# Sums of expert rows on TensorE, weight pieces into the slot that is free first, and overflow blocks in pairs

## The reference

```
# top-1 of 4 groups, then top-2 of its 8 experts; 32 experts, each 1024 -> 512 -> 1024, per layer
weights = p_group * top_p / sum(top_p)                     # two numbers for each token
y = (silu(xb @ w1[e]) * (xb @ w3[e])) @ w2[e]              # for each row given to expert e
out = sum over the token's two experts of  y * weight
x  <- LayerNorm(alpha * x + gate * out) * ln_w + ln_b      # alpha = (2 * DEPTH) ** 0.25
```

## Time and profile before

| | |
|---|---|
| median of 3 launches | 2706.59 us (2704.28 to 2708.8) |
| the profiled execution | 2711.27 us |
| its span, first to last instruction | 2709.4 us |
| PE busy | 2269.5 us (84%) |
| DVE busy | 823.1 us (30%) |
| ACT busy | 445.1 us (16%) |
| POOL busy | 352.8 us (13%) |
| mean granted clock of PE | 0.916 of full |

### The profile page before, as it was taken

How to read it: one execution, slowest core, us unless ns; L and a number is a source line. 1 busy time by engine, 2 the same in 40 slices (tenths; PEclk the granted TensorE clock), 3 DMA queues, 4 the chain that set the end, 5 groups by cost and what they waited for, 6 DMA issues and landing times.

```text
span 2709.4 us, 28307 instructions
## 1 busy us (share of the span) xinstructions
PE 2269.5 (84%) x10288; PEld 1147.0 (42%) x10288; DVE 823.1 (30%) x1648; ACT 445.1 (16%) x956; POOL 352.8 (13%) x341
## 2 busy tenths in 40 slices
PE   7989999998958898999940999998958898998920
PEld 3555458884543343433310444443543343433410
DVE  2764135554342011111139201102351111110147
ACT  2201234441211111111111100000111110111111
POOL 0000123221210000000015000001210000000025
PEclk8999999999978999999975999998968998999965
DMA  9861000003255989899852301102065989899743
GB/s 388 324 241 36 0 1 2 2 2 111 75 213 231 421 358 422 344 420 414 334 194 97 88 23 46 46 0 78 31 265 223 422 362 416 345 420 421 311 173 149
DMA packets 135164, 572.21 MB, mean 211 GB/s; under 512 B 24153, under 2 KB 49913, under 8 KB 82554
## 3 DMA queue, kind: packets, MB, share of 16 engines
q1 hardware_dynamic: 121786, 536.92, 50.3%
q0 software_dynamic: 13248, 33.57, 3.2%
HBM read 549.47 MB, written 35.65 MB: 216 GB/s over the span
## 4 chain that ended last, share of the span: by engine, by line
PE 63%; DMA 15%; DVE 11%; SPq 5%; issue 3%; ACT 1%; POOL 1%; POOLq 0%; DVEq 0%; ACTq 0%
PE bank L966 14%; PE bank L1038 12%; DMA bigA<-in_moe_w 9%; PE bank L988 8%; PE bank L606 7%; PE bank L876 4%; PE bank L898 4%; SPq L392 4%; PE bank L709 3%; DMA bigC<-in_moe_w 2%; DVE lnwb L1365 2%; PE bank L563 2%; DVE bigA L1781 2%; DVE bigA L1783 2%; SPq L508 2%
## 5 line engine op out<-in xcount | busy, mean ns | idle before, releaser
L966 PE MATMUL bank<-bigA,bigB 128*32 128x512 f32 (+2 forms) x1920 | 476.1, 624 | 28.7 <-DMA bigA<-in_moe_w 25.4
L1038 PE MATMUL bank<-bigB,bigA 128*128 128x512 f32 x768 | 331.6, 595 | 4.9 <-DMA bigA<-in_w_in_odd 4.9
L606 PE MATMUL bank<-bigC,bigB 128*128 128x512 f32 (+3 forms) x768 | 291.8, 535 | 0.4 <-ACT bigB L1075 0.4
L988 PE MATMUL bank<-bigA,bigB 128*32 128x512 f32 (+2 forms) x1040 | 268.1, 608 | 18.9 <-DMA bigA<-in_moe_w 9.7
L966 PEld LDWEIGHTS bank<-bigA,bigB 128*32 128x32 f32 (+2 forms) x1920 | 166.3, 143 | 273.3 <-issue 268.3
L966 PE MATMUL bank<-bigC,bigB 128*32 128x512 f32 (+2 forms) x768 | 244.8, 631 | 32.1 <-DMA bigA<-in_moe_w 15.3
L1038 PEld LDWEIGHTS bank<-bigB,bigA 128*128 128x128 f32 x768 | 146.5, 191 | 189.3 <-issue 189.3
L606 PEld LDWEIGHTS bank<-bigC,bigB 128*128 128x128 f32 x768 | 142.0, 192 | 127.5 <-issue 119.4
L1075 ACT ACTIVATE bigB<-bank,small 128x128 f32<-128x128 f32 x288 | 106.6, 460 | 475.5 <-PE bank L563 475.5
L1915 POOL TENSOR_TENSOR bigA<-bigA,lnwb 128x1024 f32<-128x1024 f32 x32 | 81.9, 2558 | 700.6 <-ACT bigA L1203 700.6
L1931 POOL DMA_INDIRECT y_rows<-bigB,ints x44 | 44.3, 1007 | 966.4 <-DVE bigB L1738 966.4
(11 more groups left out here) (263 smaller groups left out, 2293.0 us busy)
## 6 DMA issues: line engine op xcount, KB each, us to landing
bigA<-in_moe_w SPq DMA_DIRECT2D x288, 1024.0 KB, 24.1
bigC<-in_moe_w SPq DMA_DIRECT2D x96, 1024.0 KB, 16.7
bigA<-in_ada_w SPq DMA_DIRECT2D x40, 1024.0 KB, 7.8
bigA<-y_rows SPq DMA_DIRECT2D x16, 1024.0 KB, 4.8
bigA<-in_w_in_odd SPq DMA_DIRECT2D x24, 512.0 KB, 5.5
bigA<-in_ada_w SPq DMA_DIRECT2D x4, 2048.0 KB, 12.4
bigA<-in_x SPq DMA_DIRECT2D x16, 512.0 KB, 11.1
bigC<-in_w_in_even SPq DMA_DIRECT2D x4, 2048.0 KB, 13.7
```

The lines of the kernel that those rows point to most:

```text
L606: last = mm(bank(n % 3)[:, 0:w], uT[:, k, t * P:(t + 1) * P], wring[:, g % 2, k, at_:at_ + w], start=(k == 0), stop=(k == KC - 1))
L966: last = mm(bank(m)[at_:at_ + w, :], xT[:, j, KC // 2 * h + k, at_:at_ + w], w13_at[SLOT_OF[m, h, q][0]][:, k, :], start=(h == 0 and k == ...
L988: last = mm(bank(6 + n)[at_:at_ + w, :], gT[:, 2 * h + k, at_:at_ + w], w2_at[SLOT_OF[2, h, q][0]][:, k, n * 512:(n + 1) * 512], start=(h ...
L1038: last = mm(bank(3 * half + m), wc[:, j, m, k, :], u1T[:, k, half * 512:(half + 1) * 512], start=(k == 0), stop=(k == KC - 1))
```

## The change

1. **Slots.** A piece goes to the slot that comes free first by the plan, no longer to slot n % 16. `BEFORE[n]` is the piece that held it, and SP waits for the end of that one. The order of the pieces stays.
2. **Sums on PE.** The gate is multiplied into the rows before they are scattered: DVE alone takes both halves of a block's result from PSUM, times `gate`. In the tail PE forms alpha * hback + weight0 * row0 + weight1 * row1 in PSUM, by six matmuls a tile: against alpha times the identity (`alpha_i`) and against diagonal tiles of the weights (`share`), which POOL makes by 16 instructions at the start of each expert loop. DVE takes the statistics from PSUM, ACT normalises from PSUM, and DVE instead of POOL does the product with `ln_w` and the sum with `ln_b` (`affine`).
3. **Order of the tail of layer 0.** The transposes and the modulation of tile t - 2 are put in after the sum of tile t (`stream_T`), where they stood behind all sums on ACT and DVE. They use banks 0 to 3 of PSUM.
4. **Overflow loop.** 12 turns with one test on every engine, SP too; a turn would take two blocks.
5. **SP** issues the first two loads of `hback` before its overflow loop, and behind it waits for the last scatters itself instead of for POOL.

```diff
-SLOT_OF = {piece: (n % SLOTS, n // SLOTS) for n, piece in enumerate(PIECES)}
+def freed(piece):
+    m, h, q = piece
+    return (LAST[q], 2 * m + h) if m < 2 else (LAST[q] + 1, 4)
+
+SLOT_OF, BEFORE, FILLS, _held = {}, {}, [0] * SLOTS, []
+for _n, _piece in enumerate(PIECES):
+    _slot = _n
+    if _n >= SLOTS:
+        _, _, _slot, BEFORE[_n] = _held.pop(0)
+    SLOT_OF[_piece] = (_slot, FILLS[_slot])
+    FILLS[_slot] += 1
+    _held = sorted(_held + [(freed(_piece), _n, _slot, _piece)])
...
-            with eng.Fori(0, (OVER + 1) // 2) as i:
-                for j in range(2):
-                    with eng.If(2 * i + j < n_over):
+            with eng.Fori(0, OVER // 2) as i:
+                with eng.If(2 * i < n_over):
+                    for j in range(2):
                         block_(i + NB // 2, j)
...
-                        m_was, h_was, q_was = PIECES[n - SLOTS]
+                        m_was, h_was, q_was = BEFORE[n]
...
+                for t in range(2):
+                    load(hback[:, t], h_dram[l][t * P:(t + 1) * P, :], f"pair_in{t}")
-                with sp.Fori(0, OVER) as o:
-                    with sp.If(o < n_over):
+                with sp.Fori(0, OVER // 2) as i:
+                    with sp.If(2 * i < n_over):
...
-                sp.wait_ge(S("rows_out"), l + 1)
+                for j in range(2):
+                    sp.wait_ge(S(f"y_out{j}"), 16 * (NB // 2) * (l + 1))
...
@@ tensor @@
+            def combined(l, t):
+                if t == 0:
+                    pe.wait_ge(S("share_ok"), l + 1)
+                pe.wait_ge(S(f"pair_in{t % 2}"), 32 * (NT // 2 * l + t // 2 + 1))
+                if t >= 2:
+                    pe.wait_ge(S("nrm"), NT * (2 * l + 1) + t - 1)
+                for n in range(2):
+                    cols_n = slice(n * 512, (n + 1) * 512)
+                    dst = bank(4 + 2 * (t % 2) + n)
+                    mm(dst, alpha_i[:, :], hback[:, t % 2, cols_n], start=True, stop=False)
+                    for k in range(2):
+                        last = mm(dst, share[:, k, t, :], pair[:, t % 2, k, cols_n], start=False, stop=(k == 1))
+                last.then_inc(S("comb"), 1)
...
             for t in range(NT):
-                pe.wait_ge(S("ln"), NT + t + 1)
+                combined(0, t)
                 if t >= 2:
-                    pe.wait_ge(S("tile_a"), NT + t - 1)
-                    pe.wait_ge(S("tile_d"), NT + t - 1)
-                transposes(hh[:, t], 4 + 2 * (t % 2)).then_inc(S("tile_T"), 1)
+                    stream_T(t - 2)
...
@@ scalar @@
-                    go(yo[:, j, 0:512], bank(6), ACT.Copy).then_inc(S(f"y_ev{l}"), 1)
...
@@ vector @@
-                    v.tensor_copy(yo[:, j, 512:1024], bank(7)).then_inc(S(f"y_ev{l}"), 1)
+                    for n in range(2):
+                        v.tensor_tensor(yo[:, j, n * 512:(n + 1) * 512], bank(6 + n), gate[:, 1, n * 512:(n + 1) * 512], MUL)\
+                            .then_inc(S(f"y_ev{l}"), 1)
...
-                    V(v.tensor_scalar(z, pair[:, j, 0, :], wts[:, 0, t:t + 1], None, MUL))
-                    V.wait()
-                    V(v.scalar_tensor_tensor(z, pair[:, j, 1, :], wts[:, 1, t:t + 1], z, MUL, ADD))
-                    V.wait()
-                    V(v.tensor_tensor(z, z, gate[:, 1, :], MUL))
-                    V.wait()
-                    v.scalar_tensor_tensor(z, hback[:, j], ALPHA, z, MUL, ADD).then_inc(S("comb"), 1)
...
             for t in range(NT):
-                dve.wait_ge(S("tile_T"), NT + t + 1)
-                modulated(u1T[:, :, t * P:(t + 1) * P], 4 + 2 * (t % 2), mod_of(1, 0), "tile_d")
+                combined(0, t)
+                if t >= 2:
+                    stream_T(t - 2)
+                affine(0, t)
...
@@ gpsimd @@
                 gather(1, tok[:, 1:2])
+                for k in range(2):
+                    for t in range(NT):
+                        last = pool.tensor_scalar(share[:, k, t, :], ident, wts[:, k, t:t + 1], None, MUL)
+                last.then_inc(S("share_ok"), 1)
```

124 lines of the change are left out of this document (73 added, 51 removed).

## The result

The changed kernel takes **2561.8 us** (median of 4 runs, 2561.2 to 2566.1) where the kernel before takes 2707.4 (4 runs, 2704.3 to 2708.8): a ratio of 0.947, with an interval of 0.945 to 0.948. That is 145.6 us less; 132 were forecast, and 2561.8 lies in the range of 2552 to 2604. The profiled execution took 2561.2 us with a span of 2559.4.

What follows compares the result with a forecast made beforehand. PE was taken to bound the loops, idling 41.5 us a layer for weights, and DVE the tails. Gains of 56 (loops), 36.4 and 40 (tails) sum to 132 us, from 2706.6 to 2575, range 2552 to 2604.

Steps and rivals of the forecast that it cites:

- The holes in the loop: Expert loops: four stretches with DMA nearly idle, 36 us in layer 0, all gone once pieces take the first free slot.
- The carried table: Layer 0's expert loop: event times computed by recurrences from trace rows, with old and new slot releases; loop ends 1379 and 1350.
- the term of 28 us a layer: Expert loops: gain from the new slots, 29 us carried, taken as 28; 56 us for two layers, from 36 to 80.
- The bound of 18 us: Expert loops: lower bound of the slots' gain per layer, if each gather and scatter costs the queues twice as much.
- Rival D: Expert loops: gathers starve in always-full queues and the kernel is slower than before; 2785 at 39 us landing time; chance 0.02.
- rival A: Expert loops: holes close but little comes of it, 10 us for both layers; 2621 us; chance 0.12.
- The cover for what moved into the loop: Expert loops: DVE's extra 15 us and POOL's 9.6 us of diagonal tiles hide and cost nothing; uncovered, 10 us a layer.
- The pace: Tails: time per tile falls from 10.84 us to 6.1, or 6.3 in layer 0; bounds 5.9 and 7.0.
- The chain 2.28 + 1.3 + 2.5: Tails, one tile: statistics to ACT's product, ACT's product, then DVE's two wide instructions, with gaps; 6.1 us.
- one test less saves about a quarter, 8.7 us: Start of layer 0's tail: DVE's 12 overflow turns, 12.1 us with two tests, take 8.7 us with one.
- The write of the last tile behind it stays: End of layer 1's tail: the last tile's write after the last affine step stays, so no gain there (0 us).
- Rival B: Tails: PE's sums run at 1.2 GHz, 10.3 us each, and PE becomes the bound; 2652 us; chance 0.04.

Runs made afterwards that it cites:

- old-walk kernel: Kernel after with 12 overflow turns of two tests, SP's 24 turns, SP waiting for POOL, and rows of h loaded behind the loop; 2580.7 us (0.952).

## Why the prediction was right, point by point

**The holes in the loop: right, its size a little small.** The step "all four holes are gone" is in the row of 40 slices, and the slots alone give it. The carried table held within 1 us in all rows that were looked up but one: the last w2 piece of block 3 at 941 (trace 940.0), the last piece of all at 1330 (1330.3), the loop's end at 1350 (1349.6), and the outputs put at 921, 1063 and 1274 end at 920.4, 1063.6 and 1273.7. (By its numbers these are the outputs computed in the steps of blocks 3, 9 and 18, so those of blocks 2, 8 and 17. The exception is the 1296 of block 18: its own last w2 piece lands at 1291.1; the one that lands at 1296.1 belongs to the expert of blocks 19 to 21.) Some of this is luck, since everything began 1.8 us sooner than in the table: counted from the loop's start, the trace is 1 to 2.5 us behind it. What was mis-sized is the term of 28 us a layer, which measured 30.6 and 32.5. The carried loop was 3 us short for the kernel *before* (1379 against 1382), and I took a microsecond off the gain for it. The error was in the carried old loop alone. From its start at 833.4 the carried new loop is 516.6 us long, and measured were 518.0 and 516.2; so the difference should have been taken from the real 1382 to the carried 1350: 32. The bound of 18 us (a gather costs the queues twice) is ruled out by the loops themselves. The gathers are no slower either, 11.0 us in the median to land (10.8 before):

```profile
bigB<-h_rows,ints POOLq DMA_INDIRECT x22, 11.0
y_rows<-bigB,ints POOLq DMA_INDIRECT x21, 8.6
```

Rival D falls with that, and rival A, whose time was 2621, with the loops: the eight small waits carried, 11 us, are nine in the view of waits, 14.5.

**The cover for what moved into the loop: right.** DVE is busy 81.9 us instead of 69.2, POOL 48.9 instead of 43.1, and with the old slots the loop is as long as before.

**The pace: right in layer 1, its size a little large in layer 0.** Forecast 6.1 in layer 1 and 6.3 in layer 0, measured 6.0 in both. The chain 2.28 + 1.3 + 2.5 is in the rows. In layer 0 I let four modulations add 0.2 us; they fit in the wait for ACT. "DVE stays the bound, narrowly" is true, and narrower than put. In layer 0 PE has no pause at all between 1376 and 1412 (36.00 of 36 us, in the rows on rival B below), with 6.03 us of matmuls a tile: there DVE and PE are the bound together. Without the residual's matmuls or without the transposes the pace stays at 6.0, and DVE's chain holds it; with the chain cut short it is the loads' 5.8 in layer 1 and PE's 6.1 in layer 0; with the chain short and the transposes gone it is 5.7 in layer 0 as well. Three limits within 0.4 us of one another.

**The start of the tails: in layer 0 the walk was mis-sized.** The step "one test less saves about a quarter, 8.7 us" measured 6.15, 0.51 us a turn where the kernel before had 1.03. The old-walk kernel parts this in two: its two-test turns take 9.30 us, so the test that is gone is worth 3.15, a third. The other 3 us were in layer 0 of the kernel before (a turn of its layer 1 took some 0.8 us too), for a reason that no run shows. (The 12.1 us that the step started from are 12.34 in the row.) The first statistics came at T + 19.8 and not at T + 22.6, and with the smaller pace the tail was 68.0 us and not 72.6: this is the 4.6 us of layer 0. In layer 1 T + 7.1, T + 12.0 and T + 20.2 answer to T + 7.3, T + 12.2 and T + 19.7, and T + 68.3 to T + 68.5. The last is partly luck: a first sum of 8.2 us for 7.4 and a pace of 6.0 for 6.1 cancel, and a second execution has T + 66.7.

**The end of the program: the failed step.** "The write of the last tile behind it stays" is wrong. It took the 7.8 us behind the last affine step for the write. The write is 3.1 of them; the rest was POOL's closing drain, which starts with POOL's last instruction. POOL now has no work in the tail, and its drain ends 53.8 us before the program does. 4.8 us less, shown by the kernel that gives POOL only the last tile.

**Rival B: the clock.** It would have cost 2652. The granted clock in stretches of the tails, in order: layer 0, first sum; layer 0, seven tiles; layer 1, until the first sums; layer 1, the rest.

```profile
1364.00:1370.00 6.00, 6.00 (x15) 2.67 (x14) 0.62 (x2) 3.68 (x4) 0.00 (x0) 1.00 0.23 97
1376.00:1412.00 36.00, 36.00 (x122) 18.93 (x121) 31.34 (x63) 15.96 (x32) 0.00 (x0) 1.00 0.57 216
2492.00:2505.70 13.70, 5.69 (x7) 2.52 (x8) 0.00 (x0) 0.00 (x0) 0.00 (x0) 0.50 0.47 181
2506.00:2550.00 44.00, 39.38 (x90) 16.26 (x88) 29.21 (x49) 10.49 (x14) 0.00 (x0) 1.00 0.75 273
```

In layer 0 PE had nothing for 9.2 us and the half clock (1.2 GHz) fell on its first records behind that, those of the gate rows, so that it was over before the first sum:

```profile
1358.80:1362.30 3.50, 3.49 (x4) 1.51 (x5) 1.52 (x8) 0.00 (x0) 0.00 (x0) 0.51 0.71 227
```

In layer 1 it comes behind 12 us in which PE had nothing, and the first sum takes 8.2 us for it (7.4 forecast). From then on the clock is full to the end of PE's work, though PE waits 0.7 to 1.4 us for rows ahead of four sums. The Trainium skill, "TensorE: Matmul & The Clock Gate", section "HAM oscillation — how this bites in real kernels", has bursts with waits for data between them start at half clock each. The waits in its case are longer than those here; the traces agree with it for the pauses of 9.2 and 12 us, and in the old-walk kernel a wait of 2.06 us was followed by half clock too.

The gain of the tails was forecast by what DVE no longer does. The kernel with ln_w and ln_b on POOL narrows that down: the pace is 5.9 us with the products on either engine, so the 34 us a layer that the pace brings (7 steps from 10.83 to 6.0) come with the sums on PE. The move of the two products to DVE is worth 2.9 and 1.7 us at the ends of the tails, and 4.8 at the end of the program. The rest hangs on the walk and the order of the loads: without them the tails are 6.3 and 12.5 us longer, and the first statistics come later than in the kernel before (T + 26.2 for T + 24.8, T + 30.6 for T + 24.4), as a tile's sum now stands behind its load.

## What to carry to other kernels

A prefetch that refills its slots in turn stands at the slot that comes free last; hand the next piece the first free one, and look for short holes in the rate of a loop that seems full (36 us a layer here, of which 31 and 32 were won). When a stage's pace falls by the removal of its bound, look at the next limits too: taking away DVE's wait, a third of PE's sums or PE's transposes, one at a time, moved the pace by 0.2 us at most, and two at once by 0.3, as the other limits were within 0.4 us. A loop that is never entered still costs its turns on each engine that something waits for, here 0.5 us a turn, and one test around it takes them out (3.5 us at the start of layer 0's tail); and before the end of a program is put down to its last write, see which engine's drain ends last.

## What was not expected of the hardware

- POOL's closing drain takes 7.6 us behind POOL's last instruction (9.99 us from the start of a product of 2.34 us; 7.59 with nothing before it), where DVE's ends with its last instruction. It came out as 7.8 us from the last affine step to the end in the four kernels whose last product is POOL's (before, slots only, all on POOL, last tile on POOL), and as 3.0 to 3.1 in all others.
- A one-column instruction of DVE, 0.16 us, took 1.19 us when POOL's product of two operands in SBUF ran beside it (0.7 to 1.8 us in eleven others of that kernel's tails).
- With one test for two blocks a turn took DVE 0.51 us (6.15 / 12). With two tests it took 1.03 (12.34 / 12) in the kernel before and 0.78 (9.30 / 12) in the old-walk kernel; the difference between these two is open.
